# Two layers of a hybrid diffusion backbone: half of the expert weight transfers issued from ScalarE's queue

## The reference

```python
for l in range(2):                       # layer 0: dense mixer, layer 1: experts, latent tokens only
    h = modulate(rms(x)); p = h @ w_in[l]
    x = x + g1 * (concat([attention(p), retention(p), conv(p)]) @ w_out[l])
    h2 = modulate(rms(x))
    x = x + g2 * channel_mixer(h2)

def _moe(h, router, wg, wu, wd):         # the channel mixer of layer 1
    logits = h @ router
    top_v, top_i = lax.top_k(logits, 2)
    w = softmax(top_v)
    combine = sum(one_hot(top_i, 8) * w[..., None], axis=-2)
    for e in range(8):
        out = out + combine[..., e:e+1] * ((silu(h @ wg[e]) * (h @ wu[e])) @ wd[e])
    return out
```

## Time and profile before

| | us |
|---|---|
| median of 3 runs | 1902.57 |
| lowest, highest | 1901.24, 1903.86 |
| time of the profiled execution | 1901.73 |
| its span, first to last instruction | 1899.9 |
| PE, DVE, ACT busy, share of the span | 96%, 70%, 55% |
| granted TensorE clock, mean | 0.981 |
| bytes read from HBM | 470.26 MB |

### The profile page before, as it was taken

The page is one execution under the profiler, slowest core; times in us unless marked ns, Lnnn a source line. Parts: engine busy times, 40 slices in busy tenths (PEclk is TensorE's granted clock), DMA queues, the critical chain, the costliest instruction groups (busy, mean ns, idle before and its releaser), DMA issues.

```text
span 1899.9 us, 22920 instructions
## 1 busy us (share of the span) xinstructions
PE 1816.5 (96%) x8932; PEld 1479.3 (78%) x8932; DVE 1334.9 (70%) x1277; ACT 1049.2 (55%) x1003; POOL 116.5 (6%) x126
## 2 busy tenths in 40 slices
PE   4999989999999999887999999999999999999997
PEld 2986578888888888566888887888888888878886
DVE  2478646333333357745988888889889898888988
ACT  3233744222222144454777677777767777767764
POOL 1020800000000012310000000000000000000000
PEclk9999989999999999997999999999999999999999
DMA  8325922522332124644999998999989999999995
GB/s 293 127 89 185 345 67 72 140 93 85 100 108 86 53 103 149 217 183 144 357 334 368 361 371 318 372 357 360 379 317 374 347 351 368 334 343 359 370 359 213
DMA packets 246200, 472.82 MB, mean 249 GB/s; under 512 B 10578, under 2 KB 60596, under 8 KB 246092
## 3 DMA queue, kind: packets, MB, share of 16 engines
q1 hardware_dynamic: 242000, 468.14, 69.2%
q10 hardware_dynamic: 4092, 3.20, 0.5%
HBM read 470.26 MB, written 1.05 MB: 248 GB/s over the span
## 4 chain that ended last, share of the span: by engine, by line
PE 67%; DVE 13%; DMA 12%; ACT 5%; issue 2%; POOL 1%; SPq 0%; ACTq 0%; POOLq 0%; DVEq 0%
PE bank L543 19%; PE bank L545 19%; PE bank L544 19%; DVE parts L1737 6%; DMA raw<-in_moe_w_gate_dram 5%; ACT parts L1435 3%; DMA raw<-in_moe_w_up_dram 3%; DMA raw<-in_moe_w_down_dram 3%; PE bank L561 2%; DMA raw<-in_ada_w_dram 2%; PE bank L1047 1%; DVE parts L1722 1%; PE bank L790 1%; PE bank L779 1%; PE bank L1101 1%
## 5 line engine op out<-in xcount | busy, mean ns | idle before, releaser
L1737 DVE TENSOR_TENSOR parts<-raw,parts 128x2048 fp32r<-128x2048 f32 x336 | 764.8, 2288 | 100.2 <-ACT parts L1435 98.9
L1435 ACT ACTIVATE parts<-raw 128x2048 fp32r<-128x2048 f32 x336 | 642.9, 1919 | 240.4 <-DMA raw<-in_moe_w_up_dram 84.5
L543 PE MATMUL bank<-parts,XEr 128*128 128x512 f32 x896 | 355.9, 397 | 6.7 <-issue 2.5
L545 PE MATMUL bank<-parts,XEr 128*128 128x512 f32 x896 | 350.0, 391 | 0.0
L544 PE MATMUL bank<-parts,XEr 128*128 128x512 f32 x896 | 349.4, 390 | 0.0
L1296 ACT ACTIVATE parts<-raw 128x2048 fp32r<-128x2048 f32 (+1 forms) x62 | 113.2, 1831 | 271.0 <-PE bank L545 250.8
L1722 DVE TENSOR_TENSOR parts<-raw,parts 128x2048 fp32r<-128x2048 f32 (+1 forms) x62 | 135.8, 2194 | 137.3 <-ACT parts L1296 137.0
L543 PEld LDWEIGHTS bank<-parts,XEr 128*128 128x128 f32 x896 | 168.7, 188 | 44.0 <-issue 7.3
L545 PEld LDWEIGHTS bank<-parts,XEr 128*128 128x128 f32 x896 | 168.5, 188 | 36.2
L544 PEld LDWEIGHTS bank<-parts,XEr 128*128 128x128 f32 x896 | 168.9, 188 | 33.2
L543 PE MATMUL bank<-parts,HTr 128*128 128x512 f32 x448 | 175.0, 391 | 0.3 <-DVE parts L1737 0.2
(11 more groups left out here) (247 smaller groups left out, 2272.6 us busy)
## 6 DMA issues: line engine op xcount, KB each, us to landing
raw<-in_moe_w_gate_dram SPq DMA_DIRECT2D x112, 1024.0 KB, 6.6
raw<-in_moe_w_up_dram SPq DMA_DIRECT2D x112, 1024.0 KB, 6.9
raw<-in_moe_w_down_dram SPq DMA_DIRECT2D x112, 1024.0 KB, 6.4
raw<-in_ada_w_dram SPq DMA_DIRECT2D x28, 1024.0 KB, 8.2
more<-in_ada_w_dram SPq DMA_DIRECT2D x20, 1024.0 KB, 8.0
raw<-in_w_in_dram SPq DMA_DIRECT2D x12, 1024.0 KB, 5.1
raw<-in_ffn_w_gate_dram SPq DMA_DIRECT2D x22, 512.0 KB, 4.0
raw<-in_ffn_w_up_dram SPq DMA_DIRECT2D x22, 512.0 KB, 5.3
```

The lines of the kernel that those rows point to most:

```text
L543: nc.tensor.matmul(out, st[0], mv[0], start=start, stop=False)
L545: return nc.tensor.matmul(out, st[1], mv[0], start=False, stop=stop)
L1435: nc.scalar.activation(parts[:, n % PARTS, 0, :], raw[:, r, :], ACT.Copy).then_inc(hi_ready, 1)
L1737: return nc.vector.tensor_tensor(out, a, b, op)
```

## The change

The sync engine's loop is written out for all 336 items. It issues items 0 to 3 and then the even ones. Each odd item m from 5 on, 166 in all, is issued by ScalarE right behind the high part of item m-3, after a wait for the same count of `lo_ready` as before (item m-4's low part is done). The order of items, their slots, their semaphores and their data are the same.

```diff
+        def expert_item(m):
+
+            i, n = divmod(m, PAIR_ITEMS)
+            kind, half, g = order[n]
+            e, s = i * 2 + g // EF_SLICES, g % EF_SLICES
+            if kind == "down":
+                r0 = s * SLICE + half * 2 * P
+                rows = io["moe_w_down"][0][e, r0:r0 + 2 * P, :].rearrange("(k p) n -> p k n", p=P)
+                return raw[:, m % RAW, :].rearrange("p (k n) -> p k n", k=2), rows
+            r0 = half * 4 * P
+            rows = io["moe_w_" + kind][0][e, r0:r0 + 4 * P, s * SLICE:(s + 1) * SLICE].rearrange("(k p) n -> p k n", p=P)
+            return raw[:, m % RAW, :].rearrange("p (k n) -> p k n", k=4), rows
...
@@ expert_loads, on the sync engine
-                with sp.Fori(0, PAIRS) as i:
-                    for n, (kind, half, g) in enumerate(order):
-                        e = i * 2 + g // EF_SLICES
-                        s = g % EF_SLICES
-                        sp.wait_ge(lo_ready, i * PAIR_ITEMS + (before + n - RAW + 1))
...
-                        sp.dma_start(dst, rows).then_inc(raw_loaded[n % RAW], 16)
+                for m in range(PAIRS * PAIR_ITEMS):
+                    if m >= RAW and m % 2:
+                        continue
+                    if m >= RAW:
+                        sp.wait_ge(lo_ready, before + m - RAW + 1)
+                    dst, rows = expert_item(m)
+                    sp.dma_start(dst, rows).then_inc(raw_loaded[m % RAW], 16)
...
@@ split_expert, on the scalar engine
                 nc.scalar.activation(parts[:, n % PARTS, 0, :], raw[:, r, :], ACT.Copy).then_inc(hi_ready, 1)
+                m = i * PAIR_ITEMS + n + RAW - 1
+                if m % 2 and RAW <= m < PAIRS * PAIR_ITEMS:
+                    act.wait_ge(lo_ready, BASE + part * PAIRS * PAIR_ITEMS + m - RAW + 1)
+                    dst, rows = expert_item(m)
+                    act.dma_start(dst, rows).then_inc(raw_loaded[m % RAW], 16)
```

## The result

| | before | after |
|---|---|---|
| median of 4 runs, us | 1901.9 | 1935.67 |
| lowest, highest | 1897.55, 1903.86 | 1924.54, 1936.95 |
| span of the profiled execution | 1899.9 | 1934.0 |

The ratio is 1.0165, 95% interval 1.0143 to 1.0186. Five further runs of the change gave a median of 1928.14 us, against 1903.4 for the kernel before beside it, and 1.0138 (1.0122 to 1.0154). So the change costs 25 to 34 us by the medians (26 to 31 by the ratios), where I had forecast 4.4.

A forecast was written before the change was run, and what follows sets the result against it. The prediction took TensorE as the bound, the transfers a close second. Parts 1 to 4 and the clock summed as 0 + 1 + 0 + 2.9 + 0.5 = +4.4 us, for a median of 1907.0 us, range 1900 to 1917.

The forecast's parts named there:

- What bounds the kernel: Experts' stage: TensorE is the bound, transfers a close second; better feeding could return about 10 us.
- part 2: ScalarE's queue inside a pair: waits and issues mostly covered by waits for landings; +1 us, bounds 0 and +10.
- rival 1: Items in two queues share the DMA engines, the first of two lands later; +11 us more, 1918, mild 1912; chance 0.22.
- Part 1, the loop: Sync engine's written-out loop: at most 0.14 us saved a round; taken as 0, bounds -4.2 us and 0.
- Part 3, between the pairs: Pair borders: item 87 issued 4.6 us later behind `gathered`, covered by 0.9 us; taken as 0, bounds 0 and +1.
- Part 4, the opening: Experts' opening: item 5's uncovered wait delays `gathered` and the first product, from 896.50 to 899.35; +2.9 us.
- The clock: TensorE's restart at the opening: a longer pause ahead might lengthen the stretch at the lower clock; +0.5 us.
- The two queues: Raw transfers: by rule, queues share the same 16 DMA engines, so the change has nothing to win; no term in the sum.
- the 2 us of slack: Raw slot's round: 11.8 us allowed, 9.6 needed with the shortest transfer, so delays up to about 2 us are absorbed.

The follow-up runs named there:

- sp_all: Against the kernel before: the sync engine issues all 336 items, its loop written out, ScalarE none; 1900.69 us, 0.9988.
- change_again: The change itself run once more, unaltered, as a yardstick against the kernel before; 1928.14 us, 1.0138.
- waits_alone: Against the change: the sync engine issues all items, ScalarE keeps its 166 waits without a DMA behind them; 1907.41 us, 1.0013 to the kernel before.
- all_on_act: Against the change: ScalarE issues every item from item 8 on (328), the sync engine items 0 to 7; 1905.81 us, 1.0014 to the kernel before.
- item5_sp: Against the change: item 5 is issued by the sync engine, leaving 165 items in ScalarE's queue; 1924.04 us, 1.0116 to the kernel before.

## Why the prediction was wrong

The sign was right, the size wrong by six to eight times, and the range left the result out. Step by step:

**What bounds the kernel**: right as far as it went. TensorE was the bound, and nothing could be won beyond the 10 us of its waits. But I also took these waits as a measure of what can be lost (part 2's bound was the waits doubled, rival 1's price eight of the longest), and that doesn't follow.

**Part 1, the loop**: taken at 0; 0.9988 (0.9964 to 1.0013).

**Part 2, waits and issues in ACT's queue**: taken at +1 us, bounds 0 to +10. One queue with 328 of them costs 0.26% more than sp_all, 5 us, so half as many some 2 to 3 (an estimate; the two ratios have intervals of 0.2% each). Right in size, as far as the noise lets one tell.

**Part 3, between the pairs**: taken at 0. In the timeline of the kernel after, item 87 is issued by ACT behind `gathered`:

```profile
1153.59 0.37 ACTq L1445 DMA_DIRECT2D raw<-in_moe_w_up_dram  x1
...
1160.97 1.92 ACT L1440 ACTIVATE parts<-raw 128x2048 fp32r<-128x2048 f32 x1 [0.45 <-DVE parts L1747]
```

That is 3.9 us behind the low part that freed its slot; it landed after 5.0 us, and ACT came to it 2.4 us later still. Covered at this border, as worked out.

**Part 4, the opening**: right. The timeline of the kernel after, against the earlier trace rows:

```profile
878.57 5.51 ACT L1440 ACTIVATE parts<-raw 128x2048 fp32r<-128x2048 f32 x3
892.90 0.39 ACTq L1445 DMA_DIRECT2D raw<-in_moe_w_gate_dram  x1
893.38 1.91 ACT L1440 ACTIVATE parts<-raw 128x2048 fp32r<-128x2048 f32 x1 [9.30 <-DVE parts L1747]
...
896.72 1.49 ACT L1454 ACTIVATE XF<-bank,ada,scl 128x128 f32<-128x128 f32 x4
...
898.89 1.29 DVE L1747 TENSOR_TENSOR XEr<-XF,XEr 128x512 fp32r<-128x512 f32 x2 [3.05 <-ACT XEr L1458]
...
899.73 0.77 PE L556 MATMUL bank<-parts,XEr 128*128 128x512 f32 x1 [5.30 <-DVE XEr L1747]
```

ACT's series of high parts breaks after the third (x3), and the fourth stands 9.30 us. The first product comes at 899.73 instead of 896.50; this execution was already 0.44 later ahead of the gathering (888.72 against 888.28), so the wait costs 2.8 us (3.1 by TensorE's pause alone), for 2.9 forecast.

**The clock**: taken at +0.5 for the restart at the opening; 0 in this execution. From 899.7 to 903.3 us, against the earlier trace rows:

```profile
899.70:903.30 3.60, 3.57 (x9) 2.88 (x10) 3.60 (x3) 0.00 (x0) 0.00 (x0) 0.55 0.00 0
```

As before, some 3.3 us and 8 to 9 matmuls pass at the lower level, after a pause of 5.30 us instead of 2.15. Other executions show that this isn't fixed: in change_again's the clock was 0.50 for 4.0 us behind the restart (2.0 us lost), in waits_alone's for 4.2, and in sp_all's and all_on_act's, with the short pause, for none. What the sum missed is the lower clock later in the stage, 3.4 us (above).

**The two queues: the step that failed.** The sum had no term for them. I gave their sharing 0.22 as rival 1, priced it at +11 us more, and argued that it limits itself, since "m+1 lands no later, the bytes are the same, and a loss empties the queues, which ends the sharing". The runs show otherwise: 1.2 to 1.5%, 24 to 29 us, with the same bytes (all_on_act against the change), and 1.0%, 19 us, where the openings are alike too (all_on_act against item5_sp). Two things were wrong in it. Items are used in order, so the earlier landing of m+1 isn't worth what the delay of m costs: DVE can't go through them faster than one in 2.29 us, at 2.95 an item there is little to catch up with, and the slots behind are freed late. And the 2 us of slack was worked out with the shortest transfer, 5.35 us; with the usual 6.6 the same sum leaves 1.0 us (11.8 - 10.8), and 10.1 us to landing (the chain above) goes beyond either in one step. The DMA engines' mean busy share of 1000 to 1800 us was 0.974 before, 0.963 in the change and 0.974 in change_again: a loss doesn't empty the queues far enough to end the sharing. The Trainium skill, DMA: Bandwidth & Descriptors, section "Queues, rings and completion order", has it that each DMA engine takes turns between the queues it has work for; the trace agrees, with item 68's packets 0.32 us apart and one of item 69 between each two. The row that would have given the price wasn't in the trace of before, and I set the chance by an argument instead of by the bound that I had worked out myself: one transfer of 2.87 us against 2 us of slack.

The parts of the forecast that came true, the opening and the waits in one queue, make 5 to 6 us of the 25 to 34; the rest came from what the sum had left out.

What stays open: the share of ACT's own waits in the change, once landings are out of step (56 us of ACT's time in the change, 47 in change_again). The sum of opening (2.8 us) and single-queue waits (2 to 3 us) leaves 19 to 29 us for sharing and for what the two do together, the lower clock included; the runs don't divide these further.

## What to carry to other kernels

Where large transfers are used in the order of their issue and the DMA engines are nearly full, keep them in one queue: a second queue brings no bandwidth, and it makes the next item due share the engines with the one after. If another engine must issue, give it all of them (1.0014) and not every second one (1.0138 to 1.0165). And before a wait goes into a busy engine's queue, read what stands behind it at the openings, where its cover is missing.

## What the hardware showed that I had not expected

Packets are hardly slower with two queues: 2 KiB packets took 90.8 ns on average before, 91.7 after and 91.9 in all_on_act, which loses next to nothing; 4 KiB packets took 173.7 before, 173.5 in all_on_act and 177.6 after (all queues, 1000 to 1800 us). The 4 ns on 22528 packets of 4 KiB are under 6 us of each of the 16 engines' time in these 800 us, an estimate of the most that speed can have to do with it. Most of the loss is in which item's packets come first. GpSimd's path, on the other hand, took 1.9% in one queue: the first engine's landing came 5.2 us after the issue, where the hardware queues gave 4.9, the issue started 0.3 us behind the low part instead of 0.03, and its packets, all of 4 KiB where the other queues mostly used 2 KiB, took 179.5 ns.
